# Expert blocks of 32 tokens in four column strips, in place of 64 tokens in two

## What is computed

```python
logits = (ht @ w_router + b_router)
top_val, top_idx = lax.top_k(logits, 4)
gates = jax.nn.softmax(top_val, axis=-1)
...
hg = xblk @ w_gu[e] + b_gu[e]              # w_gu[e]: 1024 x 2048
x_glu, x_lin = hg[:, :1024], hg[:, 1024:]
x_glu = jnp.minimum(x_glu, 7.0)
x_lin = jnp.clip(x_lin, -7.0, 7.0)
act = x_glu * jax.nn.sigmoid(1.702 * x_glu) * (x_lin + 1.0)
y = act @ w_down[e] + b_down[e]            # w_down[e]: 1024 x 1024
...
out = sum over a token's experts of gate * y
```

## Time and profile before

| | us |
|---|---|
| median of 3 runs | 2867.7 |
| lowest, highest | 2866.73, 2867.71 |
| the profiled execution's own time | 2866.94 |
| its span in the profile | 2865.1 |
| PE busy | 2650.0 (92%) |
| PE weight loads, beside it | 1335.0 (47%) |
| DVE busy | 530.3 (19%) |
| ACT busy | 476.0 (17%) |
| granted PE clock, mean share | 0.953 |
| HBM read | 600.83 MB, 210 GB/s over the span |
| expert weight loads: 256 of w_gu, 128 of w_down | 1 MB each |

### The profile page before, as it was taken

One profiled execution on the slowest core, in us unless ns is written; L12 is line 12 of the kernel. 1 busy time (PEld: TensorE's weight loads), 2 busy tenths in 40 slices (PEclk: granted clock), 3 DMA queues, 4 the chain that ended last, 5 costly groups with the idle time before them and its releaser, 6 DMA issues.

```text
span 2865.1 us, 27634 instructions
## 1 busy us (share of the span) xinstructions
PE 2650.0 (92%) x10828; PEld 1335.0 (47%) x10829; DVE 530.3 (19%) x1234; ACT 476.0 (17%) x903; POOL 0.2 (0%) x4
## 2 busy tenths in 40 slices
PE   7979998999999978989999766899999999999997
PEld 2335443444444455468888545433333333333333
DVE  0011221111110011031100332321212122222222
ACT  0342123210100031131102325100000000000001
POOL 0000000000000000000000000000000000000000
PEclk9989999999999988999999757899999999999999
DMA  9713442122222214634444201499998697999895
GB/s 344 239 44 103 161 150 85 59 82 80 66 66 88 87 60 149 225 129 147 147 162 133 88 0 59 199 418 417 418 419 349 281 419 301 419 417 419 360 411 216
DMA packets 267332, 602.86 MB, mean 210 GB/s; under 512 B 10370, under 2 KB 201346, under 8 KB 234242
## 3 DMA queue, kind: packets, MB, share of 16 engines
q1 hardware_dynamic: 264896, 599.04, 55.5%
q10 hardware_dynamic: 2370, 2.88, 0.3%
HBM read 600.83 MB, written 1.05 MB: 210 GB/s over the span
## 4 chain that ended last, share of the span: by engine, by line
PE 84%; ACT 5%; DMA 4%; DVE 3%; SPq 2%; issue 1%; ACTq 0%; DVEq 0%
PE bank L287 54%; PE bank L706 28%; DMA wring<-in_w_gu 3%; ACT L838 2%; SPq L1598 2%; ACT big L838 1%; ACT tmp L838 1%; PE bank L731 1%; DVE big L1167 1%; DVE big L1161 1%; PE bank L349 0%; DMA brow<-in_brouter 0%; ACT hT L838 0%; PE bank L585 0%; DVE xT L1167 0%
## 5 line engine op out<-in xcount | busy, mean ns | idle before, releaser
L706 PE MATMUL bank<-wring,big 128*64 128x512 f32 x3456 | 767.4, 595 | 17.8 <-ACT big L838 9.1
L287 PE MATMUL bank<-hT,wring 128*128 128x256 f32 (+1 forms) x2240 | 730.3, 489 | 38.3 <-ACT hT L838 21.6
L287 PEld LDWEIGHTS bank<-hT,wring 128*128 128x128 f32 x2240 | 430.4, 193 | 336.4 <-issue 300.5
L706 PEld LDWEIGHTS bank<-wring,big 128*64 128x64 f32 x3456 | 241.2, 137 | 489.6 <-issue 443.2
L287 PE MATMUL bank<-big,wring 128*128 128x256 f32 (+1 forms) x1096 | 351.7, 483 | 27.6 <-issue 10.7
L287 PEld LDWEIGHTS bank<-big,wring 128*128 128x128 f32 x1096 | 213.0, 195 | 166.3 <-issue 130.0
L287 PE MATMUL bank<-wring,cs 128*2 128x256 f32 (+1 forms) x1152 | 262.4, 381 | 16.7 <-ACT cs L838 16.7
L838 ACT ACTIVATE big<-bank 128x256 f32<-128x256 f32 (+3 forms) x241 | 108.9, 452 | 921.0 <-PE bank L731 521.4
L287 PEld LDWEIGHTS bank<-wring,cs 128*2 128x2 f32 (+1 forms) x1152 | 92.2, 85 | 163.4 <-DMA brow<-in_brouter 16.4
L706 PE MATMUL bank<-big 64*128 64x256 f32 (+1 forms) x872 | 142.4, 466 | 5.0 <-DVE big L1164 4.5
L1164 DVE TENSOR_SCALAR big<-bank 128x512 f32<-128x512 f32 (+1 forms) x73 | 50.0, 685 | 480.7 <-PE bank L706 480.7
(11 more groups left out here) (126 smaller groups left out, 1068.9 us busy)
## 6 DMA issues: line engine op xcount, KB each, us to landing
wring<-in_w_gu SPq DMA_DIRECT2D x256, 1024.0 KB, 14.8
wring<-in_w_down SPq DMA_DIRECT2D x128, 1024.0 KB, 14.4
wring<-in_mod_w SPq DMA_DIRECT2D x48, 1024.0 KB, 11.8
wring<-in_ffn_w_up SPq DMA_DIRECT2D x44, 1024.0 KB, 5.0
wring<-in_w_ada SPq DMA_DIRECT2D x24, 1024.0 KB, 5.3
wring<-in_ffn_w_down SPq DMA_DIRECT2D x16, 1024.0 KB, 5.1
wring<-in_w_in SPq DMA_DIRECT2D x14, 1024.0 KB, 5.0
wring<-in_ev_w_in SPq DMA_DIRECT2D x12, 1024.0 KB, 11.7
```

The lines of the kernel that those rows point to most:

```text
L287: ins = pe.matmul(o, l, r, start=start, stop=stop, skip_group_check=True)
L706: ins = pe.matmul(o, l, r, start=start, stop=stop, skip_group_check=True)
```

## The change

CAP goes from 64 to 32. A block now holds 32 tokens, which are 32 columns of the array; four matmuls stand side by side in four 32-column strips, each on 256 columns of the weights (`strip(bank, q)` in place of `halves`). A bank then carries 1024 results of a token as four strips of 256 in its first 256 columns, so the tiles between the engines are [128, 256] in place of [128, 512], with half as many transposes. The scatter reads four row strips of 32 in place of two of 64. The tables are for 64 blocks in place of 49; the blocks of an expert are counted by 7 comparisons in place of 3. The ring, the loads and their waits are the same.

```diff
-CAP = 64
+CAP = 32
+Q = P // CAP
 MAXB = S * 4 // CAP + NE
...
-            def halves(bk, i):
-
-                return bk[CAP * i:CAP * i + CAP, :]
+            def strip(bk, q):
+
+                return bk[CAP * q:CAP * q + CAP, 0:S]
...
 def gather(sels, inc):
...
-                    for i in range(2):
-                        last = tt == 1 and i == 1
-                        xmm(halves(bank[7], i), SEL[:, tt, :], H2[:, tt, T2 * i:T2 * i + T2], tt == 0, tt == 1,
-                            G("m_rows") if last else inc if (tt == 0 and i == 0) else None)
+                    for q in range(Q):
+                        last = tt == 1 and q == Q - 1
+                        xmm(strip(bank[7], q), SEL[:, tt, :], H2[:, tt, S * q:S * q + S], tt == 0, tt == 1,
+                            G("m_rows") if last else inc if (tt == 0 and q == 0) else None)
...
 def bias(first=None):
-                for q in range(4):
-                    xmm(halves(bank[4 + q // 2], q % 2), OH[:, q, :], BG, True, False, first if q == 0 else None)
+                for i in range(2):
+                    for q in range(Q):
+                        xmm(strip(bank[4 + i], q), OH[:, 2 * i + q // 2, :], BG[:, S * (q % 2):S * (q % 2) + S],
+                            True, False, first if i == 0 and q == 0 else None)
...
 def gate_up(ts, e):
...
-                    for q in range(4):
...
-                        xmm(halves(bank[4 + q // 2], q % 2), kchunk(XG, t), ws[:, T2 * q:T2 * q + T2], False, t == 7, inc)
+                    for i in range(2):
+                        for q in range(Q):
...
+                            c0 = D * i + S * q
+                            xmm(strip(bank[4 + i], q), kchunk(XG, t), ws[:, c0:c0 + S], False, t == 7, inc)
...
 def down(e):
...
-                        for i in range(2):
-                            last = j == 1 and i == 1
-                            xmm(halves(bank[6], i), kchunk(AC, k), ws[:, j, T2 * i:T2 * i + T2], k == 0, k == 7,
+                        for q in range(Q):
+                            last = j == 1 and q == Q - 1
+                            xmm(strip(bank[6], q), kchunk(AC, k), ws[:, j, S * q:S * q + S], k == 0, k == 7,
...
 def scatter(inc=None):
-                for c4 in range(4):
-                    for i in range(2):
-                        c = 4 * i + c4
-                        xmm(bank[c // 2][:, S * (c % 2):S * (c % 2) + S],
-                            YK[CAP * i:CAP * i + CAP, P * c4:P * c4 + P], SGT[CAP * i:CAP * i + CAP, :],
-                            False, False, inc if c == 7 else None)
+                for i in range(2):
+                    for q in range(Q):
+                        xmm(bank[q][:, S * i:S * i + S], YK[CAP * q:CAP * q + CAP, P * i:P * i + P],
+                            SGT[CAP * q:CAP * q + CAP, :], False, False, inc if i == 1 and q == Q - 1 else None)
...
-                flip(bank[6], AV, 4, G("m_at"))
+                flip(bank[6], AV, 2, G("m_at"))
                 pe.wait_ge(G("m_rows_out"), b + 2)
-                flip(bank[7], XS, 4, G("m_x"))
+                flip(bank[7], XS, 2, G("m_x"))
...
-                A(XS, bank[7][:, :], ACT.Copy).then_inc(G("m_rows_out"), 1)
+                A(XS, bank[7][:, 0:S], ACT.Copy).then_inc(G("m_rows_out"), 1)
...
-            for i in range(2, 4):
+            for i in range(2, S // CAP):
                 ins = STT(nb, bk[:, 0:NE], float(CAP * i), nb, ALU.is_gt, ADD)
...
-            link(TT(le, cb, C("bidx").unsqueeze(2).to_broadcast([P, MAXB + 1, NE]), ALU.is_le))
+            link(TT(le, cb, C("bidx").unsqueeze(2).to_broadcast([P, MAXB, NE]), ALU.is_le))
...
-                TS(GL, bank[4][:, :], 7.0, None, ALU.min).then_inc(G("m_glu_in"), 1)
+                TS(GL, bank[4][:, 0:S], 7.0, None, ALU.min).then_inc(G("m_glu_in"), 1)
...
-                v.tensor_copy(YK, bank[6][:, :]).then_inc(G("m_yk"), 1)
+                v.tensor_copy(YK, bank[6][:, 0:S]).then_inc(G("m_yk"), 1)
```

More of the change, by code:

```diff
@@ L50 @@
 TAB = [("ident", 128), ("ones", 256), ("bd64", 128), ("rot", 128), ("cos", 256), ("sin", 256),
-       ("tri", 128), ("hmask", 128), ("rbase", 256), ("iota", 2 * CAP), ("bidx", MAXB + 1),
+       ("tri", 128), ("hmask", 128), ("rbase", 256), ("iota", P), ("bidx", MAXB),
        ("hreset", 256), ("eps", 1)]
@@ L97, in tables @@
     t["invc"] = np.broadcast_to(invc.reshape(1, -1), (P, 4 * S))
-    t["iota"] = np.broadcast_to(np.arange(2 * CAP) % CAP, (P, 2 * CAP))
-    t["bidx"] = np.broadcast_to(np.arange(MAXB + 1), (P, MAXB + 1))
+    t["iota"] = np.broadcast_to(p % CAP, (P, P))
+    t["bidx"] = np.broadcast_to(np.arange(MAXB), (P, MAXB))
     t["hreset"] = np.broadcast_to((q % HC != 0), (P, S))
@@ L249, in program @@
         H2 = big[:, 0:4, :].rearrange("p a b -> p (a b)").rearrange("p (t d) -> p t d", t=2)
[L250 to L257, removed]
+        XS = big[:, 4, 0:S]
+        XG = big[:, 5, 0:S]
+        GL = big[:, 6, 0:S]
+        LI = big[:, 7, 0:S]
+        SI = big[:, 8, 0:S]
+        AV = big[:, 9, 0:S]
+        AC = big[:, 10, 0:S]
+        YK = big[:, 11, 0:S]
         SGT = big[:, 12, 0:S]
         SEL = big[:, 12, S:S + 2 * CAP].rearrange("p (t s) -> p t s", t=2)
-        SGS = big[:, 23, 0:4 * CAP].rearrange("p (t s) -> p t s", t=2)
-        OH = big[:, 23, 4 * CAP:8 * CAP].rearrange("p (q s) -> p q s", q=4)
+        SGS = big[:, 23, 0:2 * P].rearrange("p (t s) -> p t s", t=2)
+        OH = big[:, 23, 2 * P:2 * P + 4 * CAP].rearrange("p (q s) -> p q s", q=4)
         BG = tmp[:, 1, :]
@@ L265, in program @@
         posn = big[:, 13, 0:64].rearrange("p (t e) -> p t e", t=2)
-        le3 = big[:, 22, 0:MAXB + 1]
+        le3 = big[:, 22, 0:MAXB]
         gate = big[:, 13, 64:128].rearrange("p (t e) -> p t e", t=2)
-        offt = big[:, 13, 128:128 + MAXB + 1]
+        offt = big[:, 13, 128:128 + MAXB]
         lg = big[:, 13, 192:256].rearrange("p (t e) -> p t e", t=2)
@@ L273, in program @@
         rt = big[:, 13, 416:512]
[L274 to L277, removed]
+        le = big[:, 14:18, :].rearrange("p a b -> p (a b)").rearrange("p (b e) -> p b e", e=NE)
+        le2 = big[:, 18:22, :].rearrange("p a b -> p (a b)").rearrange("p (b e) -> p b e", e=NE)
         MOE = {}
@@ L742, in gate_up @@
                     ws = wslot(t, e)
-                    for q in range(4):
[L744 to L748, removed]
-                        xmm(halves(bank[4 + q // 2], q % 2), kchunk(XG, t), ws[:, T2 * q:T2 * q + T2], False, t == 7, inc)
+                    for i in range(2):
+                        for q in range(Q):
+                            inc = None
+                            if t == 7 and q == Q - 1:
+                                inc = G("m_lin") if i else G("m_glu")
+                            elif t < 7 and i == 1 and q == Q - 1:
+                                inc = G("moe_used")
+                            c0 = D * i + S * q
+                            xmm(strip(bank[4 + i], q), kchunk(XG, t), ws[:, c0:c0 + S], False, t == 7, inc)
             def down(e):
@@ L1121, in take_act @@
                 act.wait_ge(G("m_at"), n)
-                A(AC, bank[6][:, :], ACT.Copy).then_inc(G("m_ac"), 1)
+                A(AC, bank[6][:, 0:S], ACT.Copy).then_inc(G("m_ac"), 1)
             def take_g(n):
@@ L1493, in _ @@
             link(TS(nb, bk[:, 0:NE], float(CAP), None, ALU.is_gt))
-            for i in range(2, 4):
+            for i in range(2, S // CAP):
                 ins = STT(nb, bk[:, 0:NE], float(CAP * i), nb, ALU.is_gt, ADD)
-                if i == 2:
+                if i < S // CAP - 1:
                     link(ins)
@@ L1501, in _ @@
             link(v.tensor_tensor_scan(cum, C("ones", 0, NE), nb, 0.0, MUL, ADD))
-            cb = cum.unsqueeze(1).to_broadcast([P, MAXB + 1, NE])
-            link(TT(le, cb, C("bidx").unsqueeze(2).to_broadcast([P, MAXB + 1, NE]), ALU.is_le))
+            cb = cum.unsqueeze(1).to_broadcast([P, MAXB, NE])
+            link(TT(le, cb, C("bidx").unsqueeze(2).to_broadcast([P, MAXB, NE]), ALU.is_le))
             link(v.tensor_reduce(le3, le, AX.X, ADD))
             link(TS(le3, le3, float(NE - 1), None, ALU.min))
-            v.tensor_copy(itab[:, 0, :], le3)
+            v.tensor_copy(itab[:, 0, 0:MAXB], le3)
             TS(itab[:, 1, 0:NE], cum, -1.0, None, ADD)
```

6 lines of the change are left out of this document (3 added, 3 removed).

## The result

The kernel after takes 2944.55 us (median of 4 runs, 2941.04 to 2949.22), the kernel before beside it on the same chip 2867.22 us: a ratio of 1.0271, 95% interval 1.0253 to 1.0289. The forecast was 2947 us, from 2915 to 3010. The profiled run took 2945.28 us, with a span of 2943.5 us.

A forecast was written before the change was run, and what follows sets the result against it. PE set the pace before, with loads close behind; after, loads bind. 1827 + 2.8 + 934.3 + 84 + 74 + 0.9 + 22.0 = 2945 us of span; forecast 2947 us, range 2915 to 3010.

The forecast's parts named there:

- restart at the first load: Expert stage, after the first load goes out: 4.8 - 2.5 + 0.5, giving 2.8 us.
- 12 stops: Load queue at experts of several blocks: no slot free after the first block, 7.0 us each, 84 us.
- 5 middle blocks: Experts of three or four blocks: five further extra blocks run with the load queue idle, 5 x 14.8, 74 us.
- last landing to the end: After the last weights land: 0.9 us for their matmuls and 22.0 us to the end, scatter and copy saving 2.0.
- The four stops before: Kernel before, four experts of over 64 tokens: stopped loading costs little, as PE is the bound around them.
- The block on PE: One block's PE work in the expert stage falls from 27.97 to 14.8 us, with four strips at once.
- The 0.5 us for slow followers: Within each stop: 0.5 us because the loads after the first were expected to follow it slowly.
- The clock: PE working in pulses may drop to half clock: a stop takes 5.7 us at full, 8.3 at half; 7.0 taken.
- Pairs at 81 ns: PE's weight load and matmul pairs come slower than 54 ns: blocks of 20.9 us, 2993 us; chance 0.10.
- four strips that do not run together: On PE's array only two column strips overlap: blocks of 26.5 us, 3160 us; chance 0.07.
- Faster loads: Weight loads speed up as PE reads SBUF half as long: 26.5 us an expert, 2834 us; chance 0.03.
- no slot came back early: Weight ring: some slot is given back early, so no stops, 2789 us; given no chance of its own.

The follow-up runs named there:

- experiment 2: Kernel after with every expert held to at most two blocks, five middle blocks and tokens above 64 left out: 2870.13 us.
- experiment 1: Every expert held to one block, its further tokens left out: 2791.51 us on the kernel after, 2792.53 us on the kernel before.

## Why the prediction was right, and where its terms were off

| term | forecast | measured |
|---|---|---|
| first load issued | 1827 | 1828.4 |
| restart at the first load | 2.8 | 3.7 |
| 31 experts | 934.3 | 933.7 (30.12 each) |
| 12 stops | 84 (7.0 each) | 79.6 (6.6 each) |
| 5 middle blocks | 74 | 73.9 |
| last landing to the end | 22.9 | 24.2 |
| span | 2945 | 2943.5 |

The measured column is from the issue and landing times of the 372 loads in the trace after; experiment 2 gives the two middle terms without the trace (78.6 and 74.4). The forecast came out 2.5 us above the measured median, and the largest error of a row is 4.4 us.

**The four stops before.** I read from the chain that PE sets the pace before, with the loads close behind, and wrote that the stops cost little there. With quarter loads that kernel takes 2853.7 us, so PE is the bound to within 14 us. But the stops are not cheap: without further blocks it takes 2792.5 us (experiment 1), and what lies between that and 2867 is 66 us of stops and 9 at the end. The sum did not use the price, since it built the new time up from the loads and compared it with the measured one.

**The block on PE**, 14.8 us, was right to 0.02, partly by luck: two small errors cancel. The weight records took 54 ns, as said. Gather and scatter took 2.06 us, not 1.76. The 0.3 us that I added for the loop head don't show in a block that waits for nothing (2345.52 has no idle time in front); they show in a block that waits for its weights, as 0.31 and 0.33 us of "issue" before the bias, which I take for the loop head with nothing queued behind the last slice (no row shows the queue). There they are hidden, but for the stops.

**The stop** was right in its mechanism and 0.4 us too long as a mean (6.6 against 7.0), with two errors of opposite sign: 12 x 5.7 = 68.4 us at full clock were 72, and the 15.6 us that I added for half clock were 7.6. Six of the twelve took 5.9 to 6.1 us, and six 6.6 to 8.0. The first is, by PE's timeline after:

```profile
1862.25 1.07 PE L705 MATMUL bank<-wring,big 128*32 128x256 f32 x16 [1.42 <-DMA wring<-in_w_down]
1863.77 1.07 PE L705 MATMUL bank<-tmp,big 128*32 128x256 f32 x16 [0.45 <-issue]
1864.63 1.94 PE L705 MATMUL bank<-wring,big 128*32 128x256 f32 x32
```

and by SP's, the first load after it:

```profile
1865.90 4.29 SPq L1599 DMA_DIRECT2D wring<-in_w_gu  x5
```

The last slice's matmuls start at its landing (1862.25), the bias 1.52 us later and not 0.86, since the loop head (0.45 us of "issue") stands between; the first slice is done 1.72 us after that, and the load goes out 0.41 later. From landing to issue that is 3.7 us, 0.8 more than my 2.9. The load then lands after 4.9 us, as in the earlier trace rows, but the next eleven come in 27.62 us, 2.51 each. The 0.5 us for slow followers, which I read from a stop of before where issues came 1.9 us apart, weren't there. So 6.0 in place of 5.7 at full clock.

**The clock** is the rest. The six long stops are those where PE was granted half its clock when the loads stopped or within 2 us of it, and the six short ones those with the full clock. One of each, from the stretches (granted clock third from the end):

```profile
1863.00:1866.00 3.00, 2.55 (x52) 1.67 (x48) 1.83 (x7) 0.00 (x0) 0.00 (x0) 1.00 0.00 0
2726.00:2729.00 3.00, 3.00 (x36) 1.87 (x31) 1.20 (x6) 0.00 (x0) 0.00 (x0) 0.50 0.00 0
```

Both hold the first slice and all or most of the bias: at 0.50 PE was busy all 3.00 us with 36 records, at 1.00 it did 52 in 2.55 us. Over the twelve stops the clock cost 7.6 us, the long ones' 43.6 less six times 6.0. I had put it between 0 and 31 (12 x 2.6) and taken half. In experiment 2 a stop that had half the clock from the landing on took 9.2 us, so that the cost of one stop is anything from 0 to some 3 us, by where the low level falls. Before these stops PE had worked in pulses: one slice in every 2.5 us. The other cost of the clock is in the tail. The scatter saved the 2.0 us that I gave it (from its start to the final stage's first matmul 2.10 us, 4.18 in the kernel before), but the 16 matmuls behind it took 6.44 us at a granted clock of 0.57, and 4.57 at 1.00 before:

```profile
2925.20:2931.60 6.40, 6.39 (x16) 4.91 (x16) 0.00 (x0) 5.11 (x15) 0.00 (x0) 0.57 0.00 0
```
```profile
2848.20:2852.80 4.60, 4.57 (x16) 2.38 (x16) 0.00 (x0) 4.58 (x15) 0.00 (x0) 1.00 0.00 0
```

**The rivals.** Pairs at 81 ns (2993 us) and four strips that do not run together (3160 us) both fell to the rows of the block, and to the quarter loads: 2573 us leaves no room for blocks of 20.9. The Trainium skill's 81 ns for a sustained pair of weight load and matmul at 128 columns (TensorE: Matmul & The Clock Gate, "Back-to-back issue gap") doesn't hold for these four strips: 96 such pairs, each of 256 columns, came at 54 ns each. Nor does the rule of its "Part 3: Packing small matmuls" that weight loads overlap running matmuls only when the row group differs: all four strips share the 128 rows, each of the 96 records has a weight load, and they still come at 54 ns. That this rule would undo column strips was my inference: the same part of the page lists a speed-up for them. Faster loads (2834 us) did not come: 418 GB/s in a stretch in which PE reads half as much as before. And no slot came back early (2789 us): the stops stand where SP's threshold puts them. That number is what the kernel would reach without them; experiment 1, which leaves out the extra blocks with them, gives 2791.5.

## What to carry over

Ask what the faster engine waits for before you count its gain: PE's 281 us were real, and were hidden behind weights that take 30.1 us an expert. Then ask what the change does to the stage that does bind: here a smaller block raised the number of passes over an expert's weights, and each further pass holds the ring's slots while nothing loads. To save PE work without it, keep the block at the size that the buffer's release wants and skip inside it: the halves that are left out gave 1.0% where smaller blocks lost 2.7%.

When a stop is to be priced, take it from the same kind of stop in the trace of before, whole, with the lag of the engine that frees the buffers: summing up its steps gave 5.7 against 6.0 for an engine that keeps up, and 8 in place of 11 for one that doesn't.

## What the runs showed of the hardware

- Four column strips of 32, all on the same 128 rows, each record with its own weight load, run at 54 ns a record of 256 columns in float32. Going round the four strips bank by bank, or giving each strip both of its matmuls in a row, takes the same time (2944.6 and 2945.8 us).
- In the kernel after, the first load after 3.6 to 34.9 us without one takes 4.8 to 5.4 us to land, and the eleven behind it follow at full pace at once, 2.51 us each.
- PE at one slice in 2.5 us got a granted clock of 0.77 and 0.83 on average in two experts of 30 us, going between the two levels. In the experts themselves that cost nothing; it was paid in the stops (7.6 us) and in the tail (1.9 us).
